# A decoder step on one core: the first 128 tokens through the whole trunk in f32, then the other 384

## What is computed

```python
xn = _rmsnorm(x, p['g_mix'][l])
xr, yr, ca, cb, ga, gb = _split_cols(xn @ p['w_in'][l])          # 4 x 1024 and 2 x 2048 columns
xc, rc = _causal_dwconv(xr, rnn_conv[l], p['w_rconv'][l], p['b_rconv'][l])   # 4 taps
h, h_last = _rglru(xc, rnn_h[l], p['w_r'][l], ...)              # gates, then h_t = a_t h_(t-1) + b_t
branch_a = (h * jax.nn.gelu(yr)) @ p['w_a'][l]
glu = ca * jax.nn.sigmoid(cb)
dc, cc = _causal_dwconv(glu, cm_conv[l], p['w_cconv'][l], p['b_cconv'][l])   # 31 taps
branch_b = jax.nn.silu(_layernorm(dc, ...)) @ p['w_b'][l]
merged = jax.nn.sigmoid(ga) * branch_a + jax.nn.sigmoid(gb) * branch_b
x = x + merged @ p['w_out'][l]
x = x + _peer(_rmsnorm(x, p['g_ffn'][l]), p['w_q'][l], p['keys1'][l], p['keys2'][l], u_tab, v_tab)
y = _rmsnorm(x, p['g_final'])
# _peer: 8 heads; each token picks 16 of 16384 experts per head; for each picked expert
# act = gelu(u_tab[e] . x), and the token's output gains g * act * v_tab[e] (rows of 2048)
```

## Time and profile before

| | |
|---|---|
| median of three executions | 3855.13 us (3850.53 to 3858.8) |
| the profiled execution | 3870.63 us, of which 3868.8 us are the span of the trace |
| TensorE / its weight loads busy | 3051.7 us (79%) / 1937.8 us (50%) |
| VectorE / GpSimd / ScalarE busy | 2591.0 (67%) / 1394.5 (36%) / 586.0 us (15%) |
| DMA | 1244.91 MB, 322 GB/s over the span |
| indirect transfers of u_tab and v_tab rows | 876.60 MB |

### The profile page before, as it was taken

One profiled execution on the slowest core, in us unless ns is written; L12 is line 12 of the kernel. 1 busy time (PEld: TensorE's weight loads), 2 busy tenths in 40 slices (PEclk: granted clock), 3 DMA queues, 4 the chain that ended last, 5 costly groups with the idle time before them and its releaser, 6 DMA issues.

```text
span 3868.8 us, 34526 instructions
## 1 busy us (share of the span) xinstructions
PE 3051.7 (79%) x11870; PEld 1937.8 (50%) x11870; DVE 2591.0 (67%) x3611; ACT 586.0 (15%) x1115; POOL 1394.5 (36%) x876
## 2 busy tenths in 40 slices
PE   6999989987999989888345544544179899999993
PEld 6999989975555545555112212222143334444441
DVE  2788830035777766666688887889985556665658
ACT  4444320010010000111100001222250000000000
POOL 2000000003343333324476667666612234434344
PEclk9999999989999999999676677777599999999996
DMA  4222367759899998889899999999849999999998
GB/s 125 85 84 85 97 188 241 238 191 353 327 383 391 369 380 333 321 339 355 339 410 405 407 401 404 357 383 378 316 182 350 365 408 418 421 421 421 421 422 357
DMA packets 394596, 1244.91 MB, mean 322 GB/s; under 512 B 22785, under 2 KB 268289, under 8 KB 268959
## 3 DMA queue, kind: packets, MB, share of 16 engines
q0 software_dynamic: 120720, 876.60, 56.4%
q1 hardware_dynamic: 258944, 356.03, 26.4%
q10 hardware_dynamic: 14815, 10.87, 0.9%
HBM read 1232.26 MB, written 12.00 MB: 322 GB/s over the span
## 4 chain that ended last, share of the span: by engine, by line
DMA 35%; PE 27%; DVE 20%; issue 10%; POOL 5%; ACT 1%; SPq 1%; DVEq 0%; POOLq 0%; ACTq 0%
DMA region<-in_v_tab_dram,region 26%; PE ps L1588 14%; DVE region L1418 6%; DMA region<-in_u_tab_dram,region 5%; POOL region L607 5%; DVE region L1366 4%; PE ps L1571 3%; PE ps L1573 3%; PE ps L1572 3%; DVE region L1357 1%; DMA region<-in_w_q_dram 1%; DMA region<-scores_kept 1%; DVE region L1315 1%; DVE region L1312 1%; DMA region<-in_w_in_dram 1%
## 5 line engine op out<-in xcount | busy, mean ns | idle before, releaser
L607 POOL DMA_INDIRECT region<-in_u_tab_dram,region x544 | 886.8, 1630 | 1488.5 <-DVE region L1357 578.8
L1588 PE MATMUL ps<-region,region 128*128 128x160 f32 (+1 forms) x5120 | 1208.7, 399 | 67.3 <-DMA region<-in_w_out_dram 20.1
L1588 PEld LDWEIGHTS ps<-region,region 128*128 128x128 f32 x5120 | 852.2, 194 | 415.5 <-issue 43.1
L1418 DVE SCALAR_TENSOR_TENSOR region<-region,region 128x2048 f32<-128x2048 f32 x384 | 869.5, 2287 | 105.0 <-DMA region<-in_u_tab_dram,region 104.3
L1818 PE MATMUL ps<-region,region 128*128 128x512 f32 x2048 | 890.4, 597 | 38.8 <-DMA region<-in_v_tab_dram 38.0
L1366 DVE SCALAR_TENSOR_TENSOR region<-region,region,region 128x2048 f32<-128x2048 f32 x224 | 526.8, 2352 | 560.5 <-DMA region<-in_v_tab_dram,region 548.9
L1818 PEld LDWEIGHTS ps<-region,region 128*128 128x128 f32 x2048 | 389.7, 191 | 538.9 <-issue 483.2
L607 POOL DMA_INDIRECT region<-in_v_tab_dram,region x288 | 469.5, 1630 | 423.8 <-DVE region L1366 338.6
L1766 PE MATMUL ps<-region,region 128*128 128x512 f32 x512 | 355.8, 861 | 330.3 <-DMA region<-in_v_tab_dram,region 305.7
L1766 PEld LDWEIGHTS ps<-region,region 128*128 128x128 f32 x512 | 139.2, 285 | 532.2 <-issue 505.9
L1357 DVE SCALAR_TENSOR_TENSOR region<-region,region 128x2048 f32<-128x2048 f32 x160 | 363.0, 2286 | 17.7 <-DMA region<-in_u_tab_dram,region 17.6
(11 more groups left out here) (227 smaller groups left out, 1681.0 us busy)
## 6 DMA issues: line engine op xcount, KB each, us to landing
region<-in_v_tab_dram SPq DMA_DIRECT2D x128, 1024.0 KB
region<-in_w_in_dram SPq DMA_DIRECT2D x192, 512.0 KB
region<-in_w_out_dram SPq DMA_DIRECT2D x64, 512.0 KB
region<-in_w_q_dram SPq DMA_DIRECT2D x64, 512.0 KB
region<-in_w_a_dram SPq DMA_DIRECT2D x32, 512.0 KB
region<-in_w_b_dram SPq DMA_DIRECT2D x32, 512.0 KB
region<-in_u_tab_dram,region POOLq DMA_INDIRECT x544, 12.0
region<-in_x_prompt_dram SPq DMA_DIRECT2D x7, 1024.0 KB, 16.1
```

The source lines that it names most:

```text
L607: pool.indirect_dma_start(out=slot, out_offset=None, in_=rows_ap, in_offset=bass.IndirectOffsetOnAxis(ap=idx[:, k:k + 1], axis=0)).then_in ...
L1418: stt(out=u_b[s], in0=u_b[s], scalar=1.0, in1=xn_tile(UNITS_A + u), op0=ALU.mult, op1=ALU.mult, accum_out=dots[u % 2][:, k:k + 1]).then_in ...
L1588: last = mm(outs[n][:, 0:WIDTH[g]], wide[s][:, q, n * P:(n + 1) * P], rhs(k), start=(k == 0), stop=(k == n_k - 1))
```

## The change

Group A is now the *first* 128 prompt tokens and the samples, and it goes through everything (chunk stage, branches, w_out, queries, routing) before group B's chunk stage begins. The recurrence and the convolutions of group B take their state from group A's last token, kept in `ex`. The chunk stage thus runs twice: `chunk_products(0)` over 160 columns and `chunk_products(1)` over 384, and the 32 MB of w_in that it uses are loaded twice, in pieces of 512 KB whose rows are runs of 512 bytes, as before. It works in plain f32 (`product`), with no high and low parts: `high`, `low` and `product3` are gone, and GpSimd's and ScalarE's part in them. Group B's tokens are normalized during pass 1, and turned into channels within group A's branches (`first_channels(1)`).

Group A's expert rows now start beside group B's chunk stage: of the 160 steps 32 stand in it, 4 to a chunk, 72 beside group B's branches, 22 beside w_out, 2 in the norm and 18 beside the queries. `ROWS_W` is 128, so VectorE adds 128 of group A's v_tab rows and TensorE 32, in one group instead of two (`add_group`). The states are written out during group B's branches. The diff, cut:

```diff
-ROWS_W = 6 * TOPK
+ROWS_W = 8 * TOPK
...
+STEPS_1, STEPS_2, STEPS_3, STEPS_4 = 14, 46, 118, 140
+STEPS_NORM = (STEPS_4, STEPS_4 + 2)
...
+def steps_chunk(c):
+    return STEPS_1 + (STEPS_2 - STEPS_1) * c // CC, STEPS_1 + (STEPS_2 - STEPS_1) * (c + 1) // CC
...
-            with sp.Fori(0, CC) as c:
-                block_of(0, w_in_v, c * P, (half_used[0], c * 2 + 1), (ca_done, c + 1))
...
+            def chunk_first(g, c, freed=((), (), (), ())):
+                half, done = c * 2 + (2 * CC * g + 1), c + (CC * g + 1)
+                block_of(0, w_in_v, c * P, ((half_used[0], half), *freed[0]), ((ca_done, done), *freed[1]))
+                block_of(1, w_in_v, c * P + CH, ((half_used[1], half), *freed[2]), ((cb_done, done), *freed[3]))
...
+            def chunk_weights(g, between, freed=((), (), (), ())):
+                chunk_first(g, 0, freed)
+                between()
+                chunk_rest(g, 0)
+                with sp.Fori(1, CC) as c:
+                    chunk_first(g, c)
+                    chunk_rest(g, c)
...
+            def tokens_of_b():
+                for t in range(2, NT):
+                    sp.dma_start(xt[t], x_prompt[0, (t - 1) * P:t * P, :]).then_inc(x_in[t], 16)
+
+            chunk_weights(0, tokens_of_b)
+            branch_weights(0, chunks_used(0))
...
+            chunk_weights(1, no_load, (((q_used, used - 2),), ((q_used, used - 1),), ((q_used, used),), ((q_done, HEADS + 2),)))
+            branch_weights(1, chunks_used(1))
...
-            def low(slots, n):
-                for s in slots:
-                    pool.wait_ge(hi_ready[s], n + 1)
-                    nc.gpsimd.tensor_tensor(wlo[s], wraw[s], whi_f[s], ALU.subtract).then_inc(lo_ready[s], 1)
...
-            def high(slots, use):
-
-                for s in slots:
-                    act.wait_ge(w_landed[s], use * 16 + 16)
-                    nc.scalar.activation(whi[s], wraw[s], ACT.Copy).then_inc(hi_ready[s], 1)
...
+            short_conv(0, 0)
+            recurrence_and_unit(0, 0)
+            for c in range(1, CC):
+                short_conv(0, c)
+                long_conv(0, c - 1)
+                recurrence_and_unit(0, c)
+            long_conv(0, CC - 1)
...
             norm_center(0)
-            for q in range(4):
-                k = slice(4 * q, 4 * q + 4)
-                tt(xp[:, k, COLS[1]], xh_f[:, k, COLS[1]], xl_f[:, k, COLS[1]], ALU.add).then_inc(xp_ready, 1)
             norm_scale(0)
-            merge(0, 0)
-            merge(0, 1)
-            norm_center(1)
-            merge(0, 2)
-            merge(0, 3)
-            norm_scale(1)
-            for m in range(4, DC):
+            first_channels(1)
+            for m in range(DC):
                 merge(0, m)
...
+            short_conv(1, 0)
+            recurrence_and_unit(1, 0)
+            for c in range(1, CC):
+                first, end = steps_chunk(c - 1)
+                mid = (first + end) // 2
+                expert_steps(first, mid)
+                short_conv(1, c)
+                long_conv(1, c - 1)
+                expert_steps(mid, end)
+                recurrence_and_unit(1, c)
+            long_conv(1, CC - 1)
+            expert_steps(*steps_chunk(CC - 1))
+            norm_center(1)
+            norm_scale(1)
...
-            def add_group(n):
-                dve.wait_ge(v_used, (GROUP_P, ROWS_P)[n])
-                dve.wait_ge(v_added, ROWS_W)
-                tt(xf[n], xf[n], acc[0], ALU.add).then_inc(acc_read, 1)
+            def add_group():
+                dve.wait_ge(v_used, ROWS_P)
+                tt(xf[1], xf[1], acc[0], ALU.add).then_inc(acc_read, 1)
...
-            def product3(j, pair, n, ready=None):
+            pe.wait_ge(staged_read, 3)
+
+            def product(out, pair, use, g):
 
                 for half, s in enumerate(PAIR[pair]):
-                    pe.wait_ge(lo_ready[s], n + 1)
+                    pe.wait_ge(w_landed[s], use * 16 + 16)
                     for q in range(KP):
                         k = half * KP + q
-                        if ready is not None:
-                            pe.wait_ge(ready, k + 1)
-                        hi, lo = whi[s][:, q * P:(q + 1) * P], wlo[s][:, q * P:(q + 1) * P]
-                        for a in range(2):
-                            h = slice(a * TH, (a + 1) * TH)
-                            mm(halves[j][:, a, :], hi, xh[:, k, h], start=(k == 0), stop=False)
-                            mm(halves[j][:, a, :], hi, xl[:, k, h], start=False, stop=False)
-                            last = mm(halves[j][:, a, :], lo, xh[:, k, h], start=False, stop=(k == DC - 1))
+                        last = mm(out[:, 0:WIDTH[g]], wraw[s][:, q * P:(q + 1) * P], xp[g][:, k, :],
+                                  start=(k == 0), stop=(k == DC - 1))
                     if half == 0:
                         last.then_inc(half_used[pair], 1)
                 return last
...
-            with pe.Fori(0, CC) as c:
-                pe.wait_ge(rg_ready, c + 1)
-                product3(0, 0, c * 2).then_inc(xr_done, 1)
-                pe.wait_ge(staged_read, 5)
...
+            def chunk_products(g):
+                k, m, n0 = chunk[g], PROMPT[g], CC * g
+                with pe.Fori(0, CC) as c:
+                    pe.wait_ge(xr_padded, c + (n0 + 1))
+                    product(bank(0), 0, c * 2 + USE_C[g], g).then_inc(xr_done, 1)
+                    pe.wait_ge(yg_ready, c + (n0 + 1))
+                    product(bank(2), 1, c * 2 + USE_C[g], g).then_inc(yr_done, 1)
+                    pe.wait_ge(staged_read, 5)
+                    pe.wait_ge(glu_ready, c + (n0 + 1))
+                    product(bank(6), 0, c * 2 + (USE_C[g] + 1), g).then_inc(ca_done, 1)
+
+                    pe.wait_ge(gw_landed, c * 32 + (32 * n0 + 32))
+                    pe.wait_ge(xcv_ready, c + (n0 + 2))
+                    for s, (read, done) in enumerate(((rg_ready, rgate_done), (ig_ready, igate_done))):
+                        pe.wait_ge(read, c + (n0 + 1))
+                        last = mm(bank(1 + 2 * s)[:, 0:m], gw[:, s, :], k.xcv[:, 0:m], start=True, stop=True)
+                        if g == 0:
+                            last = mm(bs(bank(1 + 2 * s)[:, m:NA]), gw[:, s, :], xc_s, start=True, stop=True)
+                        last.then_inc(done, 1)
+                    pe.wait_ge(cg_ready, c + (n0 + 1))
+                    product(bank(7), 1, c * 2 + (USE_C[g] + 1), g).then_inc(cb_done, 1)
+
+            chunk_products(0)
...
+            def branches(g):
+                done = CC * (g + 1)
+                pe.wait_ge(xr_padded, done + 1)
+                gate_a(g, 0)
+                pe.wait_ge(rg_ready, done + 1)
+                gate_b(g, 0)
+                pe.wait_ge(glu_ready, done + 1)
+                pe.wait_ge(dc_ready, done)
+                if g:
+                    for c in range(CC):
+                        last = tr(ps[0:E_N, 3, c * P:(c + 1) * P], ex[:, c, :], ident)
+                    last.then_inc(exT_done, 1)
+                pe.wait_ge(ig_ready, done + 1)
+                norm_mean(g)
+                pe.wait_ge(ha_ready, done + 1)
+                if g:
+                    pe.wait_ge(exT_read, 2)
+                    branch_a(g, 0)
+                pe.wait_ge(mean_read, g + 1)
+                norm_squares(g)
+                if g == 0:
+                    first_channels(1)
+                    branch_a(g, 0)
+                pe.wait_ge(sd_ready, g + 1)
+                branch_b(g, 0, ready=lambda k: (silu_ready, g * CC + k + 1))
+                with pe.Fori(1, PAIRS) as i:
+                    branch_pair(g, i)
+
+            branches(0)
...
             second_half(0)
-            pe.wait_ge(xp_ready, 5)
-            with pe.Fori(0, DC // 2) as i:
-                branch_pair(1, i)
+            chunk_products(1)
+            branches(1)
             second_half(1)
```

773 lines of the change are left out of this document (365 added, 408 removed).

## The result

The changed kernel takes 3905.55 us (median of four, 3898.97 to 3909.39) beside 3856.97 us for the one before (median of four, 3850.53 to 3861.26): 1.26% slower, ratio 1.0126 with the interval 1.0105 to 1.0146. I had forecast 3838 us. The profiled execution has a span of 3897.2 us, 28.4 more than that of before.

The account below looks back on a forecast made before the run. It took TensorE to bound the chunk stage and group A's branches, TensorE and DMA group B's branches, then row gathers. Terms -278 + 371 - 110 = -17 gave 3854 us profiled, 3838 us as median; range 3770 to 3905 us.

Parts of the forecast that it names:

- Pass 1: Group A's chunk loop and branches: ends at 435 us against 714, -278 us (-300 to -235).
- The matmul prices: TensorE's f32 products: a pair costs 0.271 us in pass 1, 0.659 in pass 2; 476 us against 396.
- Pass 2's chunk loop: Group B's chunk stage: 47.5 us a chunk on average for seven, 45 for the first, 377 us.
- my wait of 2 us a chunk and the longer chunks with a route: Pass 2's loop: 45 us a chunk against VectorE's 43, and 54 for the two chunks with a route.
- the two rivals on weights and clock: Late pass-2 weights: +160, 4000 us, chance 0.06; pass 1 at clock 0.71: +45, 3883 us, chance 0.06.
- pass 2 to the end of its branches: From group B's first product to its branches' end: 889 us against 518, +371 us (+345 to +450).
- The pace per pair stays, since 137 rows replace 135: Group B's branches: six pairs after the first merge keep today's 63.3 us each.
- The first paragraph of the prediction: What bounds each stage; group B's branches have both limits, TensorE 506.18 of 518 us and DMA 0.96.
- the 11 steps before the merge: Ahead of group B's first branch merge: 21 rows of 1.05 MB, 61 us at 367 GB/s.
- The tail and queries: Group B's queries give 9 us; the 55 us tail of group A's rows keeps 15, -40 us.
- The stretch of group B's first 256 rows: 32 v_tab rows on TensorE replace 64; gain taken as 61 us, of 90.6 us of waiting.
- the hand-overs of the loop: Rival: pass 2's loop at 54 us a chunk, not 47.5, from engine hand-overs; +29, 3884 us, chance 0.19.

Follow-up runs that it names:

- e1: Kernel before, with the chunk stage's three f32r matmuls made one plain f32 matmul; 3944.94 us, ratio 1.0214.
- e9: Changed kernel with the weight loads of group B's branches in pass 2 cut to a quarter; 3855.36 us, ratio 0.9990.
- e3: Changed kernel with no expert rows beside group B's chunk loop, all those steps beside its branches; 4051.89 us, ratio 1.0497.
- e2: Changed kernel with VectorE adding 96 of group A's v_tab rows and TensorE 64, as before the change; 3907.56 us, ratio 1.0108.
- e8: Changed kernel with 112 of group A's v_tab rows on VectorE and 48 on TensorE; 3905.79 us, ratio 1.0121.
- e12: Changed kernel with six expert steps per pass-2 chunk instead of four and the w_out stage's steps drawn forward; 3958.98 us, ratio 1.0261.
- e10: Changed kernel with five expert steps per pass-2 chunk instead of four, fewer beside the branches; 3926.02 us, ratio 1.0168.
- e4: Changed kernel with 10 expert steps moved from beside group B's branches to beside its queries; 3918.87 us, ratio 1.0147.
- e11: Changed kernel with five expert steps per pass-2 chunk and the w_out stage's steps drawn forward; 3922.51 us, ratio 1.0153.
- e5: Changed kernel with the last chunk's four steps behind the norm and 3 steps, not 9, in the first branch pair; 3920.06 us, ratio 1.0163.

## Why the prediction was wrong

**What held.** Pass 1: -280.6 for -278. Its parts moved against each other: the chunks take 18.3 us, TensorE's own time, where I had 20, and the loop starts at 48.7, not 42, since the parameters reached TensorE at 30.9 us, not at the 23.5 of the earlier trace rows:

```profile
30.89 1.25 PE L1543 MATMUL ps<-region,region 76*128 76x76 f32 x8 [30.89 <-DMA region<-in_state_rnn_h_dram]
...
48.70 13.21 PE L1599 MATMUL ps<-region,region 128*128 128x160 f32 x96
```

The matmul prices held: e1 shows the f32 price by itself. Pass 2's chunk loop has TensorE over 0.9 busy as I wrote, and takes 348.6 us where I had 377: its hand-overs hide fully at four steps, and my wait of 2 us a chunk and the longer chunks with a route did not come. Of the two rivals on weights and clock nothing came: TensorE waited 4.1 us for w_in in the loop, in one piece, and the granted clock is 0.99 in both loops.

**What failed.** The term "pass 2 to the end of its branches", +371, measured +421.6. Within it, from group B's first product:

| piece | forecast | after |
|---|---|---|
| chunk loop | 377 | 348.6 |
| to the first merge that TensorE needs | 111 | 150.3 |
| the last 1216 instructions | 401 | 441.2 |

The step that failed is "The pace per pair stays, since 137 rows replace 135". A pair took 69.7 us instead of 63.3, and what came in between is TensorE's wait for weights, 33.1 us where the kernel before has 3.7. The first paragraph of the prediction calls DMA 0.96 busy a limit of this stage, and the sum then leaves it out.

What is shown, and what not. e9 shows that late weights are the cause: with a quarter of their bytes the waits are gone, the stretch takes 395.1 us, and the total falls to that of the kernel before. That more rows per pair make the weights late is a part of it. Ahead of the first merge TensorE did only 1.67 pairs, beside 32 rows and with idle time between, and 115 rows share the remaining 6.33 pairs, where it had been 108. The stretch moved 161.9 MB (441.2 us at 367 GB/s); at the 382 GB/s of the kernel before these bytes need 424 us. So the bytes explain some 20 of the 37 us. For the other 17 the DMA engines were just not full: they were busy 0.96 instead of 1.00 of the time, and 367/0.96 is the same 382 GB/s. The 367 of the whole stage in the earlier trace rows would have given 441 for 401, but that would have been luck, since the last 404 us of that stage ran at 382.

The same stretch in the runs that changed its rows or its weights shows that the number of rows does not set the pace by itself. It is the last 1216 to 1218 instructions of group B's branches (e3 is left out, as TensorE waits for VectorE in it):

| kernel | rows fetched (u_tab + v_tab) | TensorE waits for weights | us |
|---|---|---|---|
| before | 64 + 44 | 3.7 | 404.0 |
| e2 | 60 + 41 | 5.6 | 401.7 |
| e8 | 60 + 47 | 16.9 | 423.9 |
| e12 | 46 + 42 | 13.9 | 412.7 |
| e10 | 53 + 48 | 20.4 | 422.6 |
| e4 | 53 + 48 | 26.0 | 434.1 |
| e11 | 53 + 48 | 29.5 | 435.3 |
| the change | 60 + 55 | 33.1 | 441.2 |
| e5 | 65 + 60 | 51.4 | 463.1 |
| e9, a quarter of the weights | 60 + 55 | 0 | 395.1 |

The waits for weights go with the time throughout. But 101 rows give 401.7 us in e2 and from 422.6 to 435.3 in e10, e4 and e11. The 13 us between e10 and e11, whose orders are the same up to the end of this stretch, show how far one profiled execution can be trusted here. The two kernels with hardly any wait add two rows of v_tab for three of u_tab, the others nearly one for one, with e8 between. That mix is a part of the change (`ROWS_W`), and the forecast had no term for it. Why it matters, whether by bunches of rows that fill the DMA engines while they idle at other times or by the way in which the queues take turns, stays open.

The 39 us in the middle are what I had left out of a chain of VectorE's work. The end of the loop on TensorE, 983.9, is not the end on VectorE, which still has rows and the last recurrence before it, so that its last long convolution starts at 997.9: 14 us. The last chunk's rows and the norm took 3.5 us more each than I had put. And the 11 steps before the merge hold one routing of 9.9 us and 19.2 us of waits for rows of v_tab, so that they run from 1055.0 to 1131.9: 77 us for my 61. That this piece cost something in the end is only argued: e5 took 12 us from it and gave more back.

**The smaller terms.** The tail and queries gave 66 us for 49: of the tail 4.6 us were left, where I had kept 15. The stretch of group B's first 256 rows gave 42 for 61. VectorE's wait for rows of u_tab fell there from 90.0 to 43.4 us, where I had asked for under 35; e2 and e8 give some 2 us there for each row of TensorE's.

**The rivals.** I had set the hand-overs of the loop at 0.19 with 3884 us. That was the right side by a mechanism that was not there, for the loop took 43.6 us a chunk. I had no case for the branches' transport, though the stage was shown with both limits at once. The rule that each DMA engine goes round its queues packet by packet (the Trainium skill, DMA: Bandwidth & Descriptors, Queues, rings and completion order) does not decide here: in the loop, where the DMA engines are 0.75 busy, the queue of small descriptors was late once; in the branches, at 0.96, weights and rows are both late, 33.1 us on TensorE and 75.8 us on VectorE, and nothing in these rows says that the small ones come off worse. Nothing excludes it either: in e4 the weights are late at 0.91 busy, and e9 would help under that rule too. No run changed the size of the descriptors alone.

What stays open: why the DMA engines are at times not full in the last 1216 instructions although TensorE waits for weights in them. VectorE waits there 42 us for ScalarE (L944 and L929), and in the same stretch of the kernel before not at all; requests for rows stand behind these waits, and may come in bunches after them. e2 has 29 us of such waits and hardly any for weights, so it cannot be this alone. No run separates it.

## What to carry to other kernels

A stage with two limits at once has no slack for a denser mix. When work beside it is moved, count what is left per unit of the main loop (here bytes per pair), not the total over the stage. The larger of the two limits is then the least that a unit can take, and not its price: 161.9 MB at 382 GB/s are 424 us, the stretch took 441, and e4 took 434 us though its bytes were fewer than those of the kernel before.

A stage that is bound by one engine takes other work for nothing only up to a sharp edge. Four steps a chunk cost 5.5 us of loop, the fifth 34 us. Over the whole loop VectorE looks 18% idle even with the fifth, but that is an average with its first chunks; in the chunks that count it was 96% busy with four already. Look for the edge in the fullest stretch of the loop.

An exchange between two stretches near their limits (rows on VectorE or on TensorE) moves time and wins none; the w_out stage's order, which filled a wait that stood ahead with work that stood behind, was worth 13 us.

## What I had not expected

The second read of 32 MB of w_in, in runs of 512 bytes beside rows of 8 KB, cost almost nothing: TensorE waited for it once, for 4.1 us (in e2 three times, 16.0 us), and its removal shortened the loop by 5.2 us. And what the DMA engines move when they are busy depends on the mix: 255 GB/s at 0.75 busy in the loop is 340 for a full one, the branches had 382 before and after the change (382 at 1.00, 367 at 0.96), and the dense stage 408 (400 at 0.98).
